# Rows of the normalised activations 524 elements long, one slot for norm scale and gate

## The reference

```python
def rmsnorm(x, w):
    xf = x.astype(jnp.float32)
    y = xf * lax.rsqrt(jnp.mean(xf * xf, axis=-1, keepdims=True) + EPS)
    return (y * w.astype(jnp.float32)).astype(x.dtype)

def modulate(h, shift, scale):
    return h * (1 + scale) + shift

def swiglu(h, wi, wo):
    a, g = jnp.split(h @ wi, 2, axis=-1)
    return (jax.nn.silu(g) * a) @ wo

# in trunk_layer, for x (and for xc where it is still needed):
x = x + 0.5 * mod[:, 2] * swiglu(modulate(rmsnorm(x, norm_w[0]), mod[:, 0], mod[:, 1]), ffn1_wi, ffn1_wo)
h = modulate(rmsnorm(x, norm_w[1]), mod[:, 3], mod[:, 4])
zq, zk, zv, zb, zc, zu, zga, zgb = jnp.split(h @ w_in, splits, axis=-1)
...
x = x + mod[:, 5] * gated_merge(o_attn, y_conv, zga, zgb, w_oa, w_ob, w_out)
x = x + 0.5 * mod[:, 8] * swiglu(modulate(rmsnorm(x, norm_w[2]), mod[:, 6], mod[:, 7]), ffn2_wi, ffn2_wo)
```

## Time and profile before

| | us |
|---|---|
| Median of 3 runs | 1981.84 |
| Lowest, highest | 1979.94, 1983.12 |
| Span of the profiled execution, first to last instruction | 1978.3 |
| Median above that span | 3.5 |
| TensorE products busy in the span | 1944.9 |
| VectorE busy | 867.2 |
| ScalarE busy | 695.4 |

### The profile page before, as it was taken

One profiled execution on the slowest core, in us unless ns is written; L12 is line 12 of the kernel. 1 busy time (PEld: TensorE's weight loads), 2 busy tenths in 40 slices (PEclk: granted clock), 3 DMA queues, 4 the chain that ended last, 5 costly groups with the idle time before them and its releaser, 6 DMA issues.

```text
span 1978.3 us, 27290 instructions
## 1 busy us (share of the span) xinstructions
PE 1944.9 (98%) x10403; PEld 1587.5 (80%) x10403; DVE 867.2 (44%) x1337; ACT 695.4 (35%) x1050; POOL 92.1 (5%) x153
## 2 busy tenths in 40 slices
PE   6999999999999999999999999999999999999998
PEld 4666688887888888666668888888888889999998
DVE  4422333236665355433333226333322487666554
ACT  2422233124434324322233115333321355545543
POOL 1011100000000001111110000000000000000000
PEclk9999999999999999999999999999999999999999
DMA  8667622232222223666753222332332244446552
GB/s 300 221 220 250 234 86 97 94 85 81 74 70 64 75 94 119 233 234 224 240 192 97 96 90 80 96 95 95 96 96 95 64 129 128 141 137 191 181 190 97
DMA packets 183071, 271.17 MB, mean 137 GB/s; under 512 B 25196, under 2 KB 146268, under 8 KB 183004
## 3 DMA queue, kind: packets, MB, share of 16 engines
q1 hardware_dynamic: 164572, 203.12, 32.6%
q0 software_dynamic: 18432, 67.12, 10.1%
HBM read 269.16 MB, written 1.05 MB: 137 GB/s over the span
## 4 chain that ended last, share of the span: by engine, by line
PE 94%; DVE 4%; DMA 1%; ACT 0%; issue 0%; POOL 0%; SPq 0%; DVEq 0%; ACTq 0%
PE ps L440 29%; PE ps L442 28%; PE ps L441 28%; PE ps L464 4%; DVE T L1086 1%; DVE hL L1093 1%; PE ps L540 1%; PE ps L681 1%; PE ps L554 1%; PE ps L499 1%; DVE wL L1016 1%; PE ps L476 1%; DMA xin<-in_ctx 0%; PE ps L493 0%; PE ps L495 0%
## 5 line engine op out<-in xcount | busy, mean ns | idle before, releaser
L1016 DVE TENSOR_TENSOR wL<-raw,wH 128x1024 fp32r<-128x1024 f32 x364 | 442.4, 1224 | 668.5 <-ACT wH L804 666.9
L440 PE MATMUL ps<-hH,wH 128*128 128x512 f32 (+1 forms) x1984 | 714.8, 360 | 1.2 <-DVE hL L1348 0.9
L442 PE MATMUL ps<-hH,wL 128*128 128x512 f32 (+1 forms) x1984 | 703.6, 355 | 0.0
L441 PE MATMUL ps<-hL,wH 128*128 128x512 f32 (+1 forms) x1984 | 702.2, 354 | 0.0
L804 ACT ACTIVATE wH<-raw 128x1024 fp32r<-128x1024 f32 x364 | 383.1, 1058 | 685.0 <-PE ps L442 680.4
L440 PEld LDWEIGHTS ps<-hH,wH 128*128 128x128 f32 x1984 | 374.9, 189 | 97.6 <-issue 45.7
L442 PEld LDWEIGHTS ps<-hH,wL 128*128 128x128 f32 x1984 | 374.9, 189 | 53.9
L441 PEld LDWEIGHTS ps<-hL,wH 128*128 128x128 f32 x1984 | 375.3, 189 | 50.0
L440 PE MATMUL ps<-GH,wH 128*128 (+2 forms) x704 | 256.6, 365 | 0.0
L441 PE MATMUL ps<-GL,wH 128*128 (+2 forms) x704 | 256.6, 365 | 0.0
L442 PE MATMUL ps<-GH,wL 128*128 (+2 forms) x704 | 256.6, 365 | 0.0
(11 more groups left out here) (138 smaller groups left out, 1393.3 us busy)
## 6 DMA issues: line engine op xcount, KB each, us to landing
raw<-in_ffn_wi SPq DMA_DIRECT2D x176, 512.0 KB, 3.6
raw<-in_ffn_wo SPq DMA_DIRECT2D x88, 512.0 KB, 3.5
adaA<-in_w_ada POOLq DMA_DIRECT2D x64, 512.0 KB, 4.7
adaB<-in_w_ada POOLq DMA_DIRECT2D x64, 512.0 KB, 4.7
raw<-in_w_in SPq DMA_DIRECT2D x60, 512.0 KB, 3.9
raw<-in_w_out SPq DMA_DIRECT2D x16, 512.0 KB, 3.6
ada0b<-in_w_ada SPq DMA_DIRECT2D x4, 1024.0 KB, 13.6
raw<-in_w_in SPq DMA_DIRECT2D x32, 128.0 KB, 2.7
```

Of the source, the lines that this page charges most:

```text
L440: mm(dst, wa, ra, start=start, stop=False, **kw)
L441: mm(dst, wa, rb, start=False, stop=False, **kw)
L442: return mm(dst, wb, ra, start=False, stop=stop, **kw)
L1016: tt(wL[:, s, :], raw[:, s, :], wH[:, s, :].bitcast(F32), ALU.subtract).then_inc(lo_done, 1)
```

## The change

The rows of hH and hL get 12 more elements, which nothing reads or writes: all accesses still name columns 0 to 511 or 0 to 255. normA and gateH lose their index over sub-layers, and every sub-layer writes and reads the same slot. No instruction, wait or transfer is added or removed; addresses in SBUF change, those of hL and of all tiles declared after it too.

```diff
+H_ROW = TOK + 12
...
-        hH = sb("hH", [P, DC, TOK], F32R)
-        hL = sb("hL", [P, DC, TOK], F32R)
+        hH = sb("hH", [P, DC, H_ROW], F32R)
+        hL = sb("hL", [P, DC, H_ROW], F32R)
...
-        normA = sb("normA", [P, 3 * DEPTH, DC, 2])
-        gateH = sb("gateH", [P, 3 * DEPTH, DC, 2])
+        normA = sb("normA", [P, DC, 2])
+        gateH = sb("gateH", [P, DC, 2])
...
-                mark(stt(normA[:, v, ks], mod[:, mi + 1, ks], 1.0,
+                mark(stt(normA[:, ks], mod[:, mi + 1, ks], 1.0,
...
-                        stt(T[:, m % 2, cs], X[:, m, cs], normA[:, v, m, hf:hf + 1], ps[4][:, cs],
+                        stt(T[:, m % 2, cs], X[:, m, cs], normA[:, m, hf:hf + 1], ps[4][:, cs],
...
-                mark(ts(gateH[:, r - 1], mod[:, mi], 0.5, None, ALU.mult))
+                mark(ts(gateH[:], mod[:, mi], 0.5, None, ALU.mult))
...
-                        stt(X[:, m, cs], ps[bank_of(m)][:, cs], gateH[:, r - 1, m, hf:hf + 1], X[:, m, cs],
+                        stt(X[:, m, cs], ps[bank_of(m)][:, cs], gateH[:, m, hf:hf + 1], X[:, m, cs],
```

## The result

The changed kernel takes 1989.53 us (median of 5 runs, 1987.45 to 1990.87) against 1981.7 us before: ratio 1.0039, 95% interval 1.0028 to 1.0051. It is slower by about 8 us, where 14 us less was forecast. The span of its profiled execution is 1985.8 us, 7.5 us more than before.

A forecast was written before the change was run, and what follows sets the result against it. TensorE bounds the kernel: product count times start spacing. Terms -9.5 + 0 - 5.3 + 1.1 - 0.6 = -14.3 us on the 1978.3 us span give 1964.0, runs about 1968; range 1934 to 2002.

The forecast's parts named there:

- the second rival (no dependence): Placement does not separate the tiles; something unseen does, such as each stage's surroundings: 1982 us; chance 0.21, cancelling effects included.
- Narrow h: 256-column products on hH and hL: spacing falls from 120.4 to 115.7 ns over 2016 products, -9.5 us.
- Wide G and narrow G, Q, Y: Products on the G, Q and Y tiles, moved to offset 64: -5.3 us, +1.1 us and -0.6 us.
- half a step: Fall assumed for 512-column G products, -3.3 ns on 1584, as a highest value is likelier to fall: -5.3 us.
- The single slots, the writing of the longer rows, the loads: normA and gateH slots, VectorE and ScalarE row writers, transfers: 0 each; bound for the writers 1.2 us.
- Wide h: 512-column products on hH and hL: a mixture of offsets leaves 226.8 ns on average, 0 us; bounds -28.3 and +28.3.
- the disturbed stretch of the earlier trace: 512-column h products after an interruption by adaLN products: 231.3 ns over 8 intervals before settling at 226.8.
- The argument used on G: 512-column G had the highest steady spacing, 233.0 ns, and a highest value is likelier to fall than rise: -5.3 us.
- The rival "slower": 512-column h products never settle with new offsets at every row, staying near 231 to 233.5 ns: up to +18.8 us, 2001; chance 0.32.

The follow-up runs named there:

- the grid: Probe without the model: products over all 16 x 16 pairs of high-row and low-row offsets in 16-byte steps; no wide pair below 226.7 ns, wide mean 231.8.
- h_at_160: Kernel with one slot each and 512-element rows, plus a 96-byte tile between hL and raw, putting all h rows at offset 160: 2001.83 us, ratio 1.0105.
- the last gain: Narrow G and h of the last stages moved to offset 192, against the one-slot kernel with G, Q, Y at offset 0: 1966.06 us, ratio 0.9931.

## Why the prediction was wrong

The bound was read rightly: what moved is TensorE's spacing, and the spacings explain the time to within half a microsecond, with the two differences of the clock, 1.7 and 1.6 us, cancelling by luck. The prediction's spacings from rounded starts (233.5 and 233.0, 120.4, 113.6) lie within 0.4 ns of the exact ones (233.3, 120.0, 113.3), which changes nothing in its sum. That placement matters was right too, and the second rival (no dependence) is out, though what spoke for it, Y and G at one offset with two narrow spacings, is unexplained. The Trainium skill says that TensorE never waits on anyone (SBUF — State Buffer, "Who interferes with whom"). Read as the prediction reads it, that the spacing could not depend on an address, this does not hold here: up to 10 ns of 227 hang on it in a program with no other engine at work. Whether TensorE waits for another engine is a different question, which these runs don't touch. The Trainium skill gives the columns' time plus about 2.5 ns (TensorE: Matmul & The Clock Gate, "Back-to-back issue gap") as the gap of isolated products, with nothing for the weight load; no placement of this sequence, in which every product has its own weight load, reached it, and the nearest was 6.7 ns above the columns' time.

By steps:
- Narrow h, forecast -9.5 us: -3.8. Right in sign, and 2.5 times too large; the value taken, 115.7, was the middle of two other tiles' values, both of which lie below the mean over placements, 118.1.
- Wide G and narrow G, Q, Y, forecast -5.3, +1.1 and -0.6 us: -7.0, +2.3 and -0.8. Right in sign and near in size, with luck in the size: no row of before stood at offset 64, and half a step was a guess.
- The single slots, the writing of the longer rows, the loads: nothing, as forecast. The slots alone gained their 6 us by moving G.
- Wide h is the step that failed, the line that ends "I take 0": the spacing rose from 227.7 to 231.8 ns, and the term measured +17.3 us, more than the whole sum. The value rested on the mean of all losses seen (12.9 ns), which mixed narrow ones into a wide question. The wide rows alone gave 13.5 (h) and 20 (G, Q, Y), and the disturbed stretch of the earlier trace rows lay between; every one of them lay above steady h. The argument used on G, that an extreme value is likelier to move to the middle, had to be used on h as well: 226.8 was the lowest wide spacing in the trace, and it proved the lowest that any probe found. A change that spreads the offsets could then only raise it; it came to 231.8, which is also the mean over the 256 pairs of the grid.

The rival "slower" was the case that came, at 40% of its price. Its value of 233.5 was Y's, too high for a mixture, and its mechanism was half right. Offset 0 is the fast place, but not because a rhythm needs time to settle: each row of after has its own steady spacing from 228.9 to 234.5 when it runs alone, and h_at_160 shows the loss without any change of row. The range held the time (1989.5 in 1934 to 2002), but it is wide, and the forecast of a gain was wrong.

## What to carry to other kernels

Where products with a weight load each follow one another without a wait, read the spacing of starts tile by tile before moving anything in SBUF: a tile that is the fastest of its width is likely to lose by a new place, one that is the slowest to gain. In a kernel of this form, put wide rows at a multiple of 256 bytes from the weights, with rows and weights moved together by multiples of 64 bytes only (64 and 192 were tried), and look for the place of narrow rows with a probe. A probe of pure products gave the full kernel's steady wide spacings to about 0.1 ns; away from offset 0 it can land in another rhythm than the kernel, as narrow Y and G did, so measure the kernel too. And look at the granted clock afterwards: some two fifths of the last gain, 4.9 of 11.6 us, were lost to it. Padding rows to break an alignment is no rule of thumb: here it broke the one that was fast for wide rows.

## What the runs showed of the hardware

- The spacing of float32r products, each with its own 128 x 128 weight load, depends on where the moving row lies against the weights: 226.7 to 236.7 ns for 512 columns with equal offsets in steps of 16 bytes, 113.3 to 120.0 for 256. With equal offsets the pattern repeats at 256 bytes.
- Away from offset 0 one placement can have more than one steady spacing: 234.6 and 230.0 ns at 208 bytes, 117.8 and 113.3 narrow at 64. At offset 0 every stretch with 128 weight columns had 226.7 and 120.0.
- At half clock the loss was not there: in the trace of after, eight wide h products near 37 us start 426 or 427 ns apart in seven intervals, on long rows, which is the columns' time of 512 at 1.2 GHz, 426.7.
- A place of 3.4 us at half clock in the serial part of a norm cost 1.6 us each time, three times in one trace.
- The least loss above the columns' time found was 13.3 ns at widths of 320, 384, 448 and 512 (146.7, 173.3, 200.0, 226.7 ns) and 6.7 ns at 256 (113.3). Of the four offsets 0, 64, 128 and 192, the best differs by width: 64 for 448, 0 for 512, 192 for 256; at 320 all four are alike.
- VectorE's and ScalarE's instructions on rows of 2096 bytes last as long as on rows of 2048 (479 ns both times; 495 against 496).
- What physically meets is open: fewer weight columns change the map but don't remove the loss at 512 columns, and the absolute place and the distance of the high from the low row count as well.
